# The value projection chunk by chunk, with the sample group's recurrence steps and a spread between its products

## The reference

```python
# branch A, latent attention
cq = rms_norm(cq, q_norm_g);  ckv = rms_norm(ckv_raw, kv_norm_g)
q = (cq @ w_uq).reshape(..., MLA_HEADS, 96)         # queries
o_lat = mla_attend(q_lat, q_rope, ckv, krope, ...)  # softmax(q k) over the latent rows
y_a = einsum('bshr,rhv->bshv', o_lat, w_uv) ...
# branch B, gated linear recurrence, for one chunk of tokens
o = einsum('btsh,bshv->bthv', A, v) + einsum('bthk,bhkv->bthv', q * exp(b), S0)
S_new = exp(bL)[..., None] * S0 + einsum('bshk,bshv->bhkv', k * exp(bL - b), v)
o_h = rms_norm(o_h, hg_norm_g)
```

## Time and profile before

| | |
|---|---|
| three timed runs | 1972.08, 1973.42, 1973.55 us |
| span of the profiled execution, first to last instruction | 1971.2 us |
| TensorE (PE) busy | 1941.0 us, 98% |
| VectorE (DVE) busy | 1355.2 us, 69% |
| ScalarE (ACT) busy | 889.4 us, 45% |
| mean granted TensorE clock over the span | 0.995 |

### The profile page before, as it was taken

The page is one execution under the profiler, slowest core; times in us unless marked ns, Lnnn a source line. Parts: engine busy times, 40 slices in busy tenths (PEclk is TensorE's granted clock), DMA queues, the critical chain, the costliest instruction groups (busy, mean ns, idle before and its releaser), DMA issues. The chain is left out here.

```text
span 1971.2 us, 42968 instructions
## 1 busy us (share of the span) xinstructions
PE 1941.0 (98%) x17826; PEld 1855.7 (94%) x17826; DVE 1355.2 (69%) x2241; ACT 889.4 (45%) x1596; POOL 85.4 (4%) x100
## 2 busy tenths in 40 slices
PE   7999999999999999999999999999999999999998
PEld 6899998988999999999988999988989999999998
DVE  5688737773379998863468876477625899889432
ACT  5464145443344455553356522354433454556322
POOL 2000001000010000000010000010000200000100
PEclk9999999999999999999999999999999999999999
DMA  5233313121232233333323332232213222333321
GB/s 171 75 99 82 82 43 107 53 67 44 65 98 86 78 99 103 108 89 89 92 76 93 80 91 66 61 90 57 72 31 97 86 86 76 107 108 94 90 89 54
DMA packets 288272, 164.29 MB, mean 83 GB/s; under 512 B 9096, under 2 KB 279920, under 8 KB 288080
## 3 DMA queue, kind: packets, MB, share of 16 engines
q1 hardware_dynamic: 284048, 152.07, 27.8%
q0 software_dynamic: 3552, 8.36, 1.4%
q10 hardware_dynamic: 480, 1.13, 0.2%
HBM read 156.86 MB, written 4.66 MB: 82 GB/s over the span
## 5 line engine op out<-in xcount | busy, mean ns | idle before, releaser
L2467 DVE TENSOR_TENSOR wlo<-raw,whi 128x1024 fp32r<-128x1024 f32 (+2 forms) x372 | 325.7, 883 | 286.1 <-ACT whi L1689 284.8
L1689 ACT ACTIVATE whi<-raw 128x512 fp32r<-128x512 f32 (+1 forms) x371 | 287.7, 783 | 431.9 <-PE acc L887 361.9
L887 PE MATMUL acc<-xh,whi 128*128 128x272 f32 x992 | 228.0, 311 | 3.5 <-DVE xl L2467 3.1
L887 PE MATMUL acc<-xl,whi 128*128 128x272 f32 x992 | 204.9, 288 | 0.0
L887 PE MATMUL acc<-xh,wlo 128*128 128x272 f32 x992 | 204.7, 288 | 0.0
L887 PEld LDWEIGHTS acc<-xh,whi 128*128 128x128 f32 x992 | 156.0, 188 | 19.4 <-issue 14.0
L887 PEld LDWEIGHTS acc<-xh,wlo 128*128 128x128 f32 x992 | 155.9, 189 | 0.0
L887 PEld LDWEIGHTS acc<-xl,whi 128*128 128x128 f32 x992 | 155.8, 188 | 0.0
L1320 PE MATMUL ring<-xb,whi 128*128 128x272 f32 x768 | 146.4, 288 | 2.2 <-ACT xf L1689 2.1
L887 PE MATMUL acc<-hh,whi 128*128 128x272 f32 x704 | 146.8, 290 | 0.0
L887 PE MATMUL acc<-hl,whi 128*128 128x272 f32 x704 | 145.2, 287 | 0.0
(11 more groups left out here) (514 smaller groups left out, 4573.1 us busy)
## 6 DMA issues: line engine op xcount, KB each, us to landing
raw<-in_w_in_dram SPq DMA_DIRECT2D x104, 512.0 KB, 4.0
raw<-in_w_up_dram SPq DMA_DIRECT2D x88, 512.0 KB, 4.0
raw<-in_w_down_dram SPq DMA_DIRECT2D x32, 512.0 KB, 4.1
raw<-in_w_o_dram SPq DMA_DIRECT2D x16, 512.0 KB, 4.1
raw<-in_w_down_dram SPq DMA_DIRECT2D x16, 384.0 KB, 3.5
raw<-in_w_pc_dram SPq DMA_DIRECT2D x16, 256.0 KB, 2.8
raw<-in_w_pb_dram SPq DMA_DIRECT2D x16, 256.0 KB, 2.7
raw<-in_w_pa_dram SPq DMA_DIRECT2D x16, 256.0 KB, 2.7
```

The costliest lines, as they stand in the source:

```text
L887: last = pe.matmul(dst[:, b * 512:b * 512 + HALF], w[:, c:c + P], x[:, k0 + a, b * HALF:(b + 1) * HALF], start=start and a == 0 and q == 0 ...
L1689: return act.activation(dst, src, ACT.Copy)
L2467: return dve.tensor_tensor(out, a, b, op)
```

## The change

The value projection goes chunk by chunk, each chunk's three products with the first unit and then with the second, and between these stand the pieces of the sample group's recurrence and `latent_rstd(1)`. `chunk_out` and `chunk_state` take a range of heads and can be called in two halves; the group is taken by the first and announced by the second. `hgrn_sums(3)` comes behind the values. ScalarE's and VectorE's orders follow. On VectorE `state_after(4)` moves behind `cql`, and the copies into `kp` wait for it.

```diff
-        def chunk_out(layer, c):
-
-            g = group(f"o{c}", layer)
+        def chunk_out(layer, c, heads=range(HH)):
+
+            if heads[0] == 0:
+                group(f"o{c}", layer)
+            g = gbank(f"o{c}")
...
-            if c == 4:
+            if c == 4 and heads[0] == 0:
                 pe.wait_ge(*at("s_load", layer, 16))
...
-            for h in range(HH):
+            for h in heads:
...
-            last.then_inc(*inc("group_ready"))
+            if heads[-1] == HH - 1:
+                last.then_inc(*inc("group_ready"))
...
-        def chunk_state(layer, c):
-            g = group(f"st{c}", layer)
-            pe.wait_ge(*group_freed(f"kt{c}", layer))
+        def chunk_state(layer, c, heads=range(HH)):
+            if heads[0] == 0:
+                group(f"st{c}", layer)
+                pe.wait_ge(*group_freed(f"kt{c}", layer))
+            g = gbank(f"st{c}")
...
             between[1] = [(hgrn_sums, 2)]
-            between[6] = [(latent_sums, 1, 4), (chunk_out, 4)]
-            between[7] = [(chunk_state, 4)]
+            between[6] = [(latent_sums, 1, 4)]
...
+            def values_of(c, n):
+                unit_ready(l, U_UV + n)
+                if (c, n) == (0, 0):
+                    pe.wait_ge(*at("lat_lo", l, 1))
+                if n == 0:
+                    group(f"v{c}", l)
+                w1, w2 = whi[(U_UV + n) % 2], wlo[(U_UV + n) % 2]
+                for q, (x, w) in enumerate(((ckvh, w1), (ckvl, w1), (ckvh, w2))):
+                    last = pe.matmul(gbank(f"v{c}")[:, :], x[:, n, c * P:(c + 1) * P], w[:, 0:512], start=n == 0 and q == 0, stop=n == 1 and q == 2)
+                if c == 3:
+                    last.then_inc(*inc("w_used"))
+                elif n == 1:
+                    last.then_inc(*inc("group_ready"))
+
+            values_of(0, 0)
+            chunk_out(l, 4, range(0, 2))
+            values_of(0, 1)
             latent_rstd(l, 1)
-            hgrn_sums(l, 3)
-            for n in range(2):
-                unit_ready(l, U_UV + n)
...
+            values_of(1, 0)
+            chunk_out(l, 4, range(2, 4))
+            values_of(1, 1)
+            values_of(2, 0)
+            chunk_state(l, 4, range(0, 2))
+            values_of(2, 1)
+            values_of(3, 0)
+            chunk_state(l, 4, range(2, 4))
+            values_of(3, 1)
             pe.wait_ge(*used_unit(l, U_UV + 1))
             pe.sem_inc(*inc("group_ready"))
+            hgrn_sums(l, 3)
             hgrn_sums(l, 4)
             hgrn_rstd(l, 1)
             latents_to_rows(l)
```

ScalarE (`value_rows(c)` waits for group v{c} and copies it to `vtm`):

```diff
             hgrn_std(2)
             next_hi(l, U_UV)
             latent_std(1)
+            next_hi(l, U_UV + 1)
...
+            value_rows(0)
             chunk_rows(4)
             hgrn_squares(4)
-            next_hi(l, U_UV + 1)
-            hgrn_std(3)
             act.wait_ge(*at("lat_done", l, 2))
             copy(cqh[:, :, :], cqn[:, :, :]).then_inc(*inc("lat_hi"))
+            value_rows(1)
+            value_rows(2)
+            value_rows(3)
+            hgrn_std(3)
             next_hi(l, U_MB)
-            for c in range(4):
-                act.wait_ge(*group_ready(f"v{c}", l))
-                copy(vtm[:, c, :], gbank(f"v{c}")[:, :]).then_inc(*group_free(f"v{c}"))
             hgrn_std(4)
```

VectorE:

```diff
             next_lo(l, U_UV)
             latent_recip(1)
+            next_lo(l, U_UV + 1)
             rope_key()
+            latent(1, cqn, V_QG)
+            hgrn_gate(4)
+            latent_lo(1, cql, cqn, cqh)
             state_after(4)
-            next_lo(l, U_UV + 1)
             hgrn_recip(3)
-            latent(1, cqn, V_QG)
-            latent_lo(1, cql, cqn, cqh)
             next_lo(l, U_MB)
-            hgrn_gate(4)
             dve.wait_ge(*at("kr_done", l, 1))
             dve.wait_ge(*at("h_og", l, 5))
+            dve.wait_ge(*group_freed("st4", l))
             for j in range(2):
                 dve.tensor_copy(kp[64:96, j, :], krT[64:96, :])
```

More of the change, by code:

```diff
@@ L1031, in chunk_out @@
                     pe.wait_ge(*group_freed(f"tree7_{k}", layer))
-            if c == 4:
+            if c == 4 and heads[0] == 0:
                 pe.wait_ge(*at("s_load", layer, 16))
-            elif c > 0:
+            elif 0 < c < 4:
                 pe.wait_ge(*group_freed(f"st{c - 1}", layer))
-            for h in range(HH):
+            for h in heads:
                 a = AT[:, c, h, :] if c < 4 else ATs[P - NS:P, h, :]
@@ L1552, in _ @@
                 with_steps(U_KR + n, 4, 4 * n, dst, n == 0, n == 1, between)
-            latent_rstd(l, 1)
-            hgrn_sums(l, 3)
-            for n in range(2):
-                unit_ready(l, U_UV + n)
[L1557 to L1560, removed]
-                for c in range(4):
[L1562 to L1566, removed]
+            def values_of(c, n):
[10 more added lines that the diff above has]
+                elif n == 1:
+                    last.then_inc(*inc("group_ready"))
+            values_of(0, 0)
+            chunk_out(l, 4, range(0, 2))
+            values_of(0, 1)
+            latent_rstd(l, 1)
+            values_of(1, 0)
[7 more added lines that the diff above has]
+            values_of(3, 1)
             pe.wait_ge(*used_unit(l, U_UV + 1))
             pe.sem_inc(*inc("group_ready"))
+            hgrn_sums(l, 3)
             hgrn_sums(l, 4)
@@ L2192, in _, with value_rows @@
             latent_std(1)
+            next_hi(l, U_UV + 1)
+            def value_rows(c):
+                act.wait_ge(*group_ready(f"v{c}", l))
+                copy(vtm[:, c, :], gbank(f"v{c}")[:, :]).then_inc(*group_free(f"v{c}"))
+            value_rows(0)
             chunk_rows(4)
             hgrn_squares(4)
-            next_hi(l, U_UV + 1)
-            hgrn_std(3)
             act.wait_ge(*at("lat_done", l, 2))
             copy(cqh[:, :, :], cqn[:, :, :]).then_inc(*inc("lat_hi"))
+            value_rows(1)
+            value_rows(2)
+            value_rows(3)
+            hgrn_std(3)
             next_hi(l, U_MB)
-            for c in range(4):
-                act.wait_ge(*group_ready(f"v{c}", l))
-                copy(vtm[:, c, :], gbank(f"v{c}")[:, :]).then_inc(*group_free(f"v{c}"))
             hgrn_std(4)
```

## The result

The changed kernel took 1975.62 us (median of 21 runs, 1974.14 to 1978.86), the kernel before beside it 1972.08 us (21 runs, 1970.39 to 1973.91). The ratio is 1.0017, 95% interval 1.0011 to 1.0023: slower by 3.5 us, about 0.2%, where 1972.3 and a gain of 1.15 us were forecast. The profiled execution took 1974.38 us with a span of 1972.6, against a span of 1971.2 before, so the pair of profiles shows 1.4 of the 3.5 us.

What follows compares the result with a forecast made beforehand. TensorE, 98% busy, was taken as the bound, with low-clock stretches in both layers. Gains of 1.05 and 2.5 us (3.55) less 2.4 for clock falls gave 1.15: 1973.42 to 1972.3 us, range 1968.5 to 1976.0.

Steps and rivals of the forecast that it cites:

- The value stage: TensorE up to the last value product: it starts at 312.45 instead of 316.02, so the stage ends 3.6 us earlier.
- it is limited by its own instructions, so the halves take 0.96 each: Value stage on TensorE: chunk_out took 1.92 us and each half was taken at 0.96.
- for which I take 0.94: Value stage on TensorE: chunk_state, 1.62 us mostly at the low clock, taken at near half plus its issue.
- last rope-key step: Start of the value stage: the rope key's last x product comes first, 0.93 us, until 303.10.
- wait and spread: At latent_rstd(1): TensorE waits 0.6 us for the accumulator rope_key frees, then the spread takes 0.53 at full clock.
- The chain behind the values: ScalarE's and VectorE's work to hgrn_scale(1) holds the queries until 319.1, leaving 1.05 us of the 3.6 in layer 0.
- The state's output hides behind this: Behind the values: st_s lands in 2.9 us, at 316.9, its copies done by 317.6 under VectorE's chain, costing nothing.
- late-landing rival: Before the queries: st_s decides from a landing 3.6 us after issue; 1974.9 to 1977.1 us, chance 0.11.
- if they end on the ktm or st_s side: Sign of being wrong: waits before the queries ended by ktm or st_s, not by VectorE's o as forecast.
- Behind the stall: After TensorE's idle time between last value product and first query: clock falls, first queries at 1.2 GHz, 1.2 us a layer.
- The clock stays high: Rival: no clock fall through the new stall before the queries; gain 3.55, 1969.9 us, chance 0.15.
- The low clock inside the value stage: Rival: the 0.6 us wait with chunk_out's halves around it lets the clock fall; 1975.5 us, chance 0.09.

Runs made afterwards that it cites:

- unsplit kernel: The changed kernel with chain and landing edits and latent_rstd(1) one place later, plus chunk_out(4) and chunk_state(4) whole; 1972.47 us, ratio 0.9998.
- the landing alone: The changed kernel with ScalarE's key-transpose drains waiting only for st_p's landing and POOL issuing st_s behind it; 1975.98 us, ratio 1.0012.
- the chain alone: The changed kernel with U_MB's hi part before v3's copy, its lo part and hgrn_recip(4) before the kp copies, hgrn_scale(1) before the memset; 1974.17 us, ratio 1.0011.

## Why the prediction was wrong, step by step

Two steps failed. The value stage was sized 1.42 us a layer too short, which took 2.84 of the 3.55 us of gain. And low clock at places that the change leaves alone stood at nothing; it added 1.94 us in the pair of profiles.

**The mis-sized term: the value stage.** The steps that failed read: "it is limited by its own instructions, so the halves take 0.96 each" and, of chunk_state, "for which I take 0.94". The last value product came 11.70 us behind the departure, not 10.28. By starts, less the product steps:

| | forecast | measured, layer 0 | excess |
|---|---|---|---|
| last rope-key step | 0.93 | 0.86 (302.53 to 303.39) | -0.07 |
| two halves of chunk_out | 1.92 | 2.39 | +0.47 |
| wait and spread | 0.6 + 0.53 | 1.42 (305.75 to 307.64, less two steps) | +0.29 |
| two halves of chunk_state | 0.94 | 1.67 | +0.73 |
| sum | | | +1.42 |

The unsplit kernel has the spread without the wait at 0.80 (308.04 to 309.31 less two steps), so the wait was worth 0.62, as forecast (0.6), although only 0.41 of it is listed as idle; the spread was 0.27 dearer. Every change from wide products to narrow ones and back costs a longer last step of the one and a slower first step of the other, 0.2 to 0.4 us a pair in these kernels (0.23 for half of `chunk_out`, 0.27 for the spread, 0.36 for half of `chunk_state`, above the times taken). The prediction had those rows (0.71 us between the start of the last value product and of the sums) and used them once, at the end of the stage, and not for the four places inside. In layer 1 the last value product came after 11.72 us: the same.

**The chain behind the values: right, but not alone.** 6.65 us forecast, 6.69 and 6.75 measured; VectorE's lo part began 2.81 us behind the last product (2.85 forecast), and in layer 0 the last wait was VectorE's `o`. But "The state's output hides behind this" failed: `st_s` landed in 2.7 to 3.4 us (2.9 forecast), and the key transposes waited 1.08 and 1.71 us for it. In the late-landing rival the landing decides from 3.6 us; at 3.4 it already ended the last listed wait of layer 1, which is one of the prediction's own signs of being wrong ("if they end on the ktm or st_s side"). The length was no luck: with the landing taken away the stage is as long as in the kernel after (+0.42 and -1.01), held by VectorE's chain. Since both waits ended within some tenths of each other, the sum was hardly touched, but the cure was: neither is worth removing alone.

**The clock: right in the value stage, wrong behind it and elsewhere.** It stayed at 1.00 through the value stage in all three profiles of the kernel after, as forecast. Behind the stall it was forecast to fall in both layers, at 1.2 us each. It did so in one of the six passages of the kernel after, for 1.1 us, and in one of the two of the landing alone, for 1.5. The size was right, the frequency was not. The Trainium skill (TensorE: Matmul & The Clock Gate, Why this matters for your kernels) puts such drops down to idle gaps between bursts, and the prediction read it so that short gaps would leave the clock alone. Five of the six passages went that way. The sixth did not: the clock fell behind 2.17 us of work in 3.40, the longest single wait in it 1.07 us. Nor did, where it fell with no gap. The third profile of the kernel after has 2.16 us of work in the same place (316.80 to 320.20) and no fall, so the busy time alone doesn't tell the two apart either.

**What no step counted.** The low stretch near 1033, 1.58 us, behind a wait of 2.05 to 2.13 us that all kernels have. It stood in all five profiled executions of the kernel after, of the chain alone and of the landing alone, and in one of the eight of the others (before three times, and one each of the other five). Nothing of the code there differs. What differs is when the program arrives: the first product behind the wait starts at 1031.26 to 1033.02 us in all six executions with the stretch, and in six of the seven without it outside that, at 1030.90 or earlier or at 1034.11. The seventh (the kernel before, third profile) starts it at 1032.59 and has none. So the time of arrival goes with the stretch in 12 of 13 executions but doesn't decide it alone; what does stays open. A change that moves everything behind it by a microsecond can gain or lose such a stretch, and this was put at nothing.

**The sum.** Forecast -3.55 + 2.4 = -1.15. Measured in the pair of profiles: -0.57 for the stage, 0 for the clock behind it, +1.94 for the two low stretches elsewhere. The -0.57 is -3.55 with 2.84 for the value stage (1.42 a layer) added, to within 0.14. The remaining 2.1 us between this pair and the medians stay in part open. The profiled execution of the kernel after is 1.2 us quicker than its median (1974.38 against 1975.62). That of the kernel before is some 0.9 slower than its own: its span of 1971.2 and the 1.8 us that lie around the span in every other profiled execution give 1973.0, against 1972.08, an estimate. That median stands between two groups of its runs (ten at 1970.39 to 1971.90, nine at 1973.19 to 1973.91), and in the three later comparisons it was 1973.04 to 1973.60. Of what makes the groups this much is known: some executions of the kernel after fall behind the stall, and some of the kernel before run at 1969.58 to 1970.79 (11 of the 64 that stood beside the experiments, mean clock 0.997), while at that same clock the kernel after takes 1975.48 to 1975.84 (5 runs). No execution of that quick group was profiled, so which low stretch it lacks stays open.

**The rivals.** "The clock stays high" happened in two of three profiles and gave no 1969.9, since the value stage took the gain. "Late landing" was the right place, with a size that made it level with VectorE's chain and no longer. The low clock inside the value stage didn't occur.

## What to carry to other kernels

When narrow matmuls are spread between wide ones, charge each place for its two switches (here 0.2 to 0.4 us), and split a block only where a half covers a wait that would cost more. Where a stall is expected, list everything that the stalled queue could be waiting for: two releasers that end within tenths of each other must be removed together: here 4.4 us of the stage for both, against 0.5 and 0.0 for either alone. For a change of 0.2% look at several profiled executions of both kernels, since one low-clock stretch more or less is as large as the effect.

## What the hardware showed unexpectedly

- A 512-column product behind narrow work needs 0.31 to 0.34 us until the next one's start instead of 0.23, and the step from a wide product to narrow work is some 0.1 longer (303.86 to 304.19).
- 3.40 us of TensorE at 100% busy ended in a low clock (305.60 in the earlier trace rows). Some 1.9 us of them were products of 32 columns, the rest of 272 and 128. The same instructions mixed with 512-column products, with TensorE busy 9.49 of 9.90 us from 302.50 to 312.40, did not.
- The same 256 KB out (`st_s`) landed in 4.9 to 6.0 us in its old place, beside a 512 KB weight load, and in 2.7 to 3.4 in its new one. Over all profiles it is 4.6 to 6.0 in the old place (four) and 2.7 to 3.8 in the new one (nine).
- Executions of one kernel in one comparison differ by up to 6.1 us (the chain alone, 1972.46 to 1978.58; the kernel before 5.4, 1969.85 to 1975.21), lower mean clocks mostly going with longer times; the three kernels with the stall removed and chunk_out in halves spread over 1.8 to 3.2 us.
